# Seven products of quarter matrices in nine MLP rounds, and norms applied late at three junctions

## The reference

```
x = x + jnp.square(jax.nn.relu(rms_norm(x, norm_mlp) @ w_ff1)) @ w_ff2      # first block; then norm_final
...
for i in range(2):                                                          # second block
    h = rmsnorm(x, norm_mixer_pre[i])
    m = diff_attention(h, ...) if i == 0 else short_conv(h, ...)
    x = x + rmsnorm(m, norm_mixer_post[i])
    h = rmsnorm(x, norm_mlp_pre[i])
    x = x + rmsnorm(jnp.square(jax.nn.relu(h @ w_up[i])) @ w_down[i], norm_mlp_post[i])
```

## Time and profile before

| | |
|---|---|
| three runs | 2018.40, 2018.44, 2020.77 us; median 2018.44 |
| profiled execution | 2018.98 us, its span 2017.2 us |
| granted TensorE clock, mean | 0.998 |
| busy: TensorE, VectorE | 1991.0, 1051.5 us |
| DMA | 188.01 MB, mean 93 GB/s |

### The profile page before, as it was taken

The page is one execution under the profiler, slowest core; times in us unless marked ns, Lnnn a source line. Parts: engine busy times, 40 slices in busy tenths (PEclk is TensorE's granted clock), DMA queues, the critical chain, the costliest instruction groups (busy, mean ns, idle before and its releaser), DMA issues.

```text
span 2017.2 us, 23414 instructions
## 1 busy us (share of the span) xinstructions
PE 1991.0 (99%) x10007; PEld 1684.6 (84%) x10007; DVE 1051.5 (52%) x981; ACT 732.3 (36%) x786; POOL 153.7 (8%) x201
## 2 busy tenths in 40 slices
PE   9999999999999999999999999999999999999998
PEld 8788888888988888898888888888888888888886
DVE  7466586655533343477777634334464565333335
ACT  5464553352323232355555423132232333132222
POOL 0100150000100000030001200000020020000000
PEclk9999999999999999999999999999999999999999
DMA  5222122133332332332222333233223233223231
GB/s 192 90 78 69 63 65 82 63 105 114 105 105 86 102 104 84 105 102 69 74 63 84 107 103 104 84 104 100 88 84 105 84 104 115 94 95 104 86 102 63
DMA packets 98982, 188.01 MB, mean 93 GB/s; under 512 B 4350, under 2 KB 16784, under 8 KB 98896
## 3 DMA queue, kind: packets, MB, share of 16 engines
q1 hardware_dynamic: 94704, 176.17, 26.4%
q0 software_dynamic: 3904, 10.51, 1.8%
q10 hardware_dynamic: 288, 0.07, 0.0%
HBM read 183.59 MB, written 2.10 MB: 92 GB/s over the span
## 4 chain that ended last, share of the span: by engine, by line
PE 89%; DVE 5%; POOL 2%; ACT 2%; issue 1%; DMA 0%; DVEq 0%; POOLq 0%; ACTq 0%
PE ps L750 52%; PE ps L948 10%; PE ps L762 5%; PE ps L720 4%; PE ps L787 4%; PE ps L1199 2%; PE ps L1193 2%; PE ps L1146 1%; PE ps L821 1%; PE ps L1052 1%; PE ps L1218 1%; PE ps L1004 1%; PE ps L976 1%; PE ps L1342 1%; DVE w_lo L1900 1%
## 5 line engine op out<-in xcount | busy, mean ns | idle before, releaser
L1900 DVE TENSOR_TENSOR w_lo<-w_raw,w_hi 128x2048 fp32r<-128x2048 f32 x126 | 288.7, 2291 | 669.6 <-ACT w_hi L1400 669.6
L1400 ACT ACTIVATE w_hi<-w_raw 128x2048 fp32r<-128x2048 f32 x126 | 241.4, 1916 | 791.7 <-PE ps L750 662.1
L750 PE MATMUL ps<-a_hi,w_hi 128*128 128x512 f32 x880 | 342.4, 389 | 0.0
L750 PE MATMUL ps<-a_lo,w_hi 128*128 128x512 f32 x880 | 342.4, 389 | 0.0
L750 PE MATMUL ps<-a_hi,w_lo 128*128 128x512 f32 x880 | 342.3, 389 | 0.0
L750 PE MATMUL ps<-w_hi,h_hi 128*128 128x512 f32 x592 | 230.3, 389 | 0.0
L750 PE MATMUL ps<-w_lo,h_hi 128*128 128x512 f32 x592 | 230.3, 389 | 0.0
L750 PE MATMUL ps<-w_hi,h_lo 128*128 128x512 f32 x592 | 230.3, 389 | 0.0
L750 PEld LDWEIGHTS ps<-a_hi,w_hi 128*128 128x128 f32 x880 | 165.2, 188 | 34.3
L750 PEld LDWEIGHTS ps<-a_hi,w_lo 128*128 128x128 f32 x880 | 165.2, 188 | 34.2
L750 PEld LDWEIGHTS ps<-a_lo,w_hi 128*128 128x128 f32 x880 | 165.2, 188 | 34.1
(11 more groups left out here) (397 smaller groups left out, 3357.5 us busy)
## 6 DMA issues: line engine op xcount, KB each, us to landing
w_raw<-in_w_ff SPq DMA_DIRECT2D x32, 1024.0 KB, 5.2
w_raw<-in_mlp_w_up SPq DMA_DIRECT2D x32, 1024.0 KB, 5.4
w_raw<-in_mlp_w_down SPq DMA_DIRECT2D x32, 1024.0 KB, 5.1
w_raw<-in_w_in SPq DMA_DIRECT2D x24, 1024.0 KB, 5.1
w_raw<-in_attn_w_qkv SPq DMA_DIRECT2D x12, 1024.0 KB, 5.2
w_raw<-in_conv_w_in SPq DMA_DIRECT2D x12, 1024.0 KB, 5.1
w_raw<-in_w_proj_gla SPq DMA_DIRECT2D x4, 1024.0 KB, 5.1
w_raw<-in_w_out SPq DMA_DIRECT2D x4, 1024.0 KB, 5.1
```

Source lines behind the costliest of these rows:

```text
L750: last = mm(ps[:, bank0 + j], left, right, start=(k == 0 and x == 0), stop=(k == QUAD * quads - 1 and x == 2), skip_group_check=halves)
L1400: nc.scalar.activation(w_hi[:, s], w_raw[:, s], ACT.Copy).then_inc(hi_ready, 1)
L1900: tt(w_lo[:, s], w_raw[:, s], w_hi[:, s].bitcast(F32), ALU.subtract).then_inc(lo_ready, 1)
```

## The change

In the first three rounds of each MLP (`FAST`) the down product of 512x1024 by 1024x1024 is made of seven products of quarters (256 tokens x 512 features by 512x512) instead of eight, 24 matmuls each, in Winograd's form of Strassen's scheme. A round then has 11 quads: 4 of the up product and 7 for the products, of which four (numbers 5, 7, 8 and 9 of a round) are sums or differences of weight quarters. VectorE makes these sums in the raw slots (`weight_sums`); two more raw slots lie in `arena` (numbers 2 and 3 of `raw_at`), and SyncE loads a round's raw quads in the order 0, 1, 2, 3, 10, 4, 5, 6. It also makes four sums of hidden quarters and seven low parts, and adds the products into y with nine instructions of 128x1024. The square moves to ScalarE. Products 7, 9 and 10 accumulate onto an earlier product in PSUM and wait until VectorE has read it. The fourth round of each MLP stays as it was. The loops are unrolled.

At h_mlp1, h_conv and h_mlp2 the second scaling falls away: the residual times the gain goes into the next stage (`weighted`), and what depends on its scale is made good later. An MLP's output grows with the square of the factor and is normalized afterwards, so GpSimd only scales that norm's epsilon (`input_scale`). In conv_in two of the three projections are multiplied by the reciprocal of the variance, a row of 512 values that goes through DRAM to reach all partitions (`gate_c`). The order of the junction, of the last block and of the next first block changes with it (`begin_unscaled`). `clear_y` is gone: the first round writes y instead of adding. Some semaphores become the shared step counter.

The core of the diff (`loaded(n, s, last)` notes that quad n is loaded into slot s when the slot's earlier reader is through, and is read until quad `last` is split; `product` is 24 matmuls: two tiles of 128 tokens by four chunks by three parts):

```diff
+        raw_at = [w_raw[:, 0], w_raw[:, 1]] + [arena[:, 2048 * k:2048 * (k + 1)].rearrange("p (a n) -> p a n", a=QUAD) for k in range(2)]
+        h_raw = [qkf[:, 2048 * u:2048 * (u + 1)].rearrange("p (half a n) -> p half a n", half=2, a=4) for u in range(2)]
+        quarter = {"11": qkf[:, 0:1024], "21": qkf[:, 1024:2048], "12": qkf[:, 2048:3072], "22": qkf[:, 3072:4096],
+                   "s3": qkf[:, 4096:5120]}
...
+            n = 0
+            while n < n_quads:
+                mine = [name for name in MLPS if ph[name].q <= n < last_q(name)]
+                if not mine:
+                    loaded(n, n % 2, n)
+                    n += 1
+                    continue
+                for k in range(4):
+                    loaded(n + k, (n + k) % 2, n + k)
+                loaded(n + 10, 2, n + 10)
+                loaded(n + 4, n % 2, n + 9)
+                loaded(n + 5, (n + 1) % 2, n + 8)
+                loaded(n + 6, 3, n + 9)
+                for k, s_ in ((7, n % 2), (8, (n + 1) % 2), (9, n % 2)):
+                    slot[n + k] = s_
+                n += FAST_Q
...
+            def input_scale(name):
+                n = junctions[name][4]
+                pool.wait_ge(sumsq_ready, stat_count(name, n, TT - 1))
+                v = var[n % 2]
+                pstep(nc.gpsimd.tensor_scalar(v, sumsq[n % 2], EPS, None, ALU.add))
+                if name == "h_conv":
+                    pstep(nc.gpsimd.tensor_scalar(eps_in, v, EPS, None, ALU.mult))
+                else:
+                    pstep(nc.gpsimd.tensor_tensor(eps_in, v, v, ALU.mult))
+                    pstep(nc.gpsimd.tensor_scalar(eps_in, eps_in, EPS, None, ALU.mult))
...
+            input_scale("h_mlp1")
             refine_tiles("h_conv")
-            pool.wait_ge(chunk_lo, 4 + 2 * 16 + 8)
+            input_scale("h_conv")
+            nc.gpsimd.memset(small[:, 243:244], 0.0).then_inc(var_made, 1)
+            pool.wait_ge(inv_made, 1)
+            dma(scale_dram.rearrange("i p -> p i"), inv_var, allow_slow_non_contiguous=True).then_inc(scale_out, 16)
+            pool.wait_ge(scale_out, 16)
...
+                    turn_tile(name, 0)
+                    tile(2, 1).then_inc(tile_done, 1)
+                    turn_tile(name, 1)
+                    tile(3, 1).then_inc(quad_done, 1)
+                    return
...
+            def begin_unscaled(name, p, js, others):
+                bank0 = 4 * (p.b % 2)
+                s0, s1 = slot_of(p, 0, 0), slot_of(p, 0, 1)
+                pe.wait_ge(hi_ready, p.q + 1)
+                pe.wait_ge(turned_hi, turn_base[name] + 3)
+                half_pass(s0, 0, bank0, 0, 0, js)
+                pe.wait_ge(turned_lo, turn_base[name] + 4)
+                half_pass(s0, 0, bank0, 0, 0, others)
+                half_pass(s0, 0, bank0, 0, 1)
+                pe.wait_ge(lo_ready, p.q + 1)
+                half_pass(s0, 0, bank0, 0, 2)
+                pe.wait_ge(hi_ready, p.q + 2)
+                half_pass(s1, 1, bank0, 0, 0)
+                pe.wait_ge(banks_free, after_block[name])
+                turn_tile(name, 2)
+                half_pass(s1, 1, bank0, 0, 1)
+                pe.wait_ge(lo_ready, p.q + 2)
+                half_pass(s1, 1, bank0, 0, 2, (0, 1))
+                turn_tile(name, 3)
+                half_pass(s1, 1, bank0, 0, 2, (2, 3))
+                pe.wait_ge(turned_hi, turn_base[name] + 7)
+                half_pass(s0, 0, bank0, 1, 0)
+                pe.wait_ge(turned_lo, turn_base[name] + 8)
+                half_pass(s0, 0, bank0, 1, 1)
+                half_pass(s0, 0, bank0, 1, 2).then_inc(quad_done, 1)
+                for x in range(3):
+                    last = half_pass(s1, 1, bank0, 1, x)
+                last.then_inc(quad_done, 1)
...
+            def fast_round(name, r, chunks):
+                p, n = ph[name], fast_q(name, r)
+                b0, b1 = 4 * (p.b % 2), 4 * ((p.b + 1) % 2)
+                added = 9 * (FAST * MLPS.index(name) + r)
+                chunk, squares_ = chunks + PRODUCTS * r, exps_at(name, r)
+                for u in range(1 if r == 0 else 0, 2):
+                    if r:
+                        pe.wait_ge(y_added, added if u else added - 1)
+                    else:
+                        pe.wait_ge(banks_free, p.b)
+                    pe.wait_ge(lo_ready, n + 2 * u + 1)
+                    multiply(a_hi, a_lo, (n + 2 * u) % 2, 0, 4 * ((p.b + u) % 2), 2, False).then_inc(quad_done, 1)
+                    pe.wait_ge(lo_ready, n + 2 * u + 2)
+                    multiply_tiles((n + 2 * u + 1) % 2, 1, 4 * ((p.b + u) % 2)).then_inc(quad_done, 1)
+                for k, op, bank, start in ((4, 0, b0, True), (5, 1, b0 + 2, True), (6, 2, b1, True), (7, 3, b0, False),
+                                           (8, 0, b1 + 2, True), (9, 1, b0, False), (10, 2, b1 + 2, False)):
+                    if k == 4:
+                        pe.wait_ge(exp_ready, squares_ + 2)
+                    if k == 6:
+                        pe.wait_ge(exp_ready, squares_ + 4)
+                    if not start:
+                        pe.wait_ge(y_added, added + {7: 1, 9: 6, 10: 7}[k])
+                    pe.wait_ge(lo_ready, n + k + 1)
+                    pe.wait_ge(chunk_lo, chunk + k - 3)
+                    product(n + k, op, bank, start)
...
+            def relu(name, r, u, c):
+                bank = 4 * ((ph[name].b + u) % 2) + 2 * c
+                n = fast_q(name, r)
+                if c == 0 and (r or u):
+                    act.wait_ge(half_made, half_number(name, r, u))
+                else:
+                    act.wait_ge(quad_done, n + 2 * u + 2)
+                dst = h_raw[u][:, :, 2 * c:2 * c + 2]
+                src = ps[:, bank:bank + 2].rearrange("p a (half n) -> p half a n", half=2)
+                step(nc.scalar.activation(dst, src, ACT.Relu))
+                nc.scalar.activation(dst, dst, ACT.Square).then_inc(exp_ready, 1)
+            def operand(name, r, chunks, k, src, op, ready=None):
+                n = fast_q(name, r)
+                if ready is not None:
+                    act.wait_ge(chunk_f32, ready)
+                if k >= 8:
+                    act.wait_ge(quad_done, n + k - 3)
+                nc.scalar.activation(op_hi[op], quarter[src], ACT.Copy).then_inc(chunk_hi, 1)
+            def fast_round(name, r, chunks, f32):
+                n, sq, f = fast_q(name, r), exps_at(name, r), f32 + 3 * r
+                split_quad(n + 2)
+                relu(name, r, 0, 0)
+                relu(name, r, 0, 1)
+                act.wait_ge(exp_ready, sq + 2)
+                operand(name, r, chunks, 4, "11", 0)
+                split_quad(n + 3)
+                operand(name, r, chunks, 5, "s3", 1, f + 1)
+                split_quad(n + 4)
+                relu(name, r, 1, 0)
+                split_quad(n + 5)
+                relu(name, r, 1, 1)
+                act.wait_ge(exp_ready, sq + 4)
+                operand(name, r, chunks, 6, "12", 2)
+                operand(name, r, chunks, 7, "11", 3, f + 2)
+                split_quad(n + 6)
+                operand(name, r, chunks, 8, "21", 0)
+                split_quad(n + 7)
+                operand(name, r, chunks, 9, "22", 1)
+                split_quad(n + 8)
+                operand(name, r, chunks, 10, "12", 2, f + 3)
+                split_quad(n + 9)
+                split_quad(n + 10)
+                split_quad(n + 11)
+                split_quad(n + 12)
...
+            def weight_sums(name, r, ks):
+                n = fast_q(name, r)
+                a, b = n % 2, (n + 1) % 2
+                if 5 in ks:
+                    dve.wait_ge(raw_full[2], 16 * raw_fill[n + 10])
+                    dve.wait_ge(raw_full[b], 16 * raw_fill[n + 5])
+                    tt(raw_at[b], raw_at[2], raw_at[b], ALU.subtract).then_inc(w_summed, 1)
+                if 7 in ks:
+                    dve.wait_ge(lo_ready, n + 5)
+                    dve.wait_ge(w_summed, sum_number(name, r, 5))
+                    tt(raw_at[a], raw_at[a], raw_at[b], ALU.add).then_inc(w_summed, 1)
+                if 8 in ks:
+                    dve.wait_ge(lo_ready, n + 6)
+                    dve.wait_ge(w_summed, sum_number(name, r, 7))
+                    tt(raw_at[b], raw_at[2], raw_at[a], ALU.subtract).then_inc(w_summed, 1)
+                if 9 in ks:
+                    dve.wait_ge(raw_full[3], 16 * raw_fill[n + 6])
+                    dve.wait_ge(lo_ready, n + 8)
+                    dve.wait_ge(w_summed, sum_number(name, r, 8))
+                    tt(raw_at[a], raw_at[3], raw_at[a], ALU.subtract).then_inc(w_summed, 1)
+            def fast_round(name, r, chunks, f32, acc):
+                p, n = ph[name], fast_q(name, r)
+                b0, b1 = 4 * (p.b % 2), 4 * ((p.b + 1) % 2)
+                sq, f, chunk = exps_at(name, r), f32 + 3 * r, chunks + PRODUCTS * r
+                added = 9 * (FAST * MLPS.index(name) + r)
+                count = [added]
```

(143 more changed lines are left out.)

464 lines of the change are left out of this document (234 added, 230 removed).

## The result

The changed kernel takes 2027.43 us (median of 7 runs, 2023.99 to 2029.02) against 2018.64 us for the kernel before (7 runs, 2017.89 to 2020.77). The ratio is 1.0042, 95% interval 1.0031 to 1.0052: slower by 0.4%, twice what a measurement of this kernel can tell. The forecast was 2023.2 us, slower, with a range of 2013 to 2034. The profiled execution took 2026.71 us with a span of 2024.9, so 7.7 us more span than before.

What follows compares the result with a forecast made beforehand. TensorE, busy 99% of the span, was taken as the bound. Span 2017.2 - 49.0 + 59.1 + 2.7 - 8.0 = 2022.0 us; 1.8 more for the profiled execution, 0.5 less for the median: 2023.2 us, range 2013 to 2034.

Steps and rivals of the forecast that it cites:

- The products and the stalls: Nine fast MLP rounds: 49.0 us of matmuls saved, 59.1 of stalls and 2.7 of restarts added, +12.9 us.
- the walk: VectorE's fixed order timed through a fast round: TensorE waits 2.77, 2.38 and 1.42 us before products three, four and six.
- Pitches of 2.20 and 1.14: VectorE in fast rounds: one instruction of 128x2048 every 2.20 us, one of 128x1024 every 1.14 us.
- (a): Rival: VectorE's backlog in fast rounds is smaller than walked, 2014 us or less; chance 0.20, half only to no change.
- (b): Rival: VectorE's backlog in fast rounds is larger, 0.84 to 1.5 us more a round, 2031 to 2037 us; chance 0.12.
- The late norms: Junctions: h_conv -2.8 us, h_mlp2 -2.8 and h_mlp1 -2.4, together -8.0, with bounds of nothing and -13.3.
- Clearing y and the rest: Dropping two memsets beside an MLP's first block is worth nothing; unrolled loops and merged semaphores cost nothing a row shows.
- part 3: Small edits, among them conv_in's scales read back through DRAM, expected hidden: cost 0, upper end 2 us.
- Rival (d): The read-back of the scales is late and stalls conv_in, 2025 to 2029 us; chance 0.04.
- rival (c): TensorE's clock falls after stalls; one product a round at 1.2 GHz costs 49 us more, 2072 us; chance 0.02.

Runs made afterwards that it cites:

- e2: The changed kernel with the four weight sums replaced by one-column memsets, so its output is wrong: 2000.64 us.
- e7: The kernel of e1 with one move, VectorE's split of quad n+6 put ahead of the first product's addition into y: 2045.51 us.
- e3: The changed kernel with VectorE's and ScalarE's instructions in a fast round reordered, no work left out, and the early reciprocal: 1980.82 us.
- e5: The kernel of e1 with the four weight sums made on GpSimd, same order and waits: 2054.47 us.
- e6: The kernel of e3 with the four weight sums made on GpSimd: 2029.74 us.
- e4: The kernel before with the late norms alone, including the scaling in conv_in with its late reciprocal, MLP rounds and clearing of y untouched: 2012.01 us.
- e1: The changed kernel with VectorE's reciprocal of the variance moved ahead of conv_in's first two splits: 2021.46 us.

## Why the prediction was right, and where it wasn't

- **The products and the stalls** (-49.0, +59.1, +2.7): +12.9 forecast, +12.2 measured; a round of 88.5, measured 88.3 to 88.6. The waits end with VectorE's splits and lie where the walk put them, but for the sixth product's, which three rounds don't have. Their lengths are others than in the walk (2.70, 0.5 and 1.1 us, or 2.70 and 2.08, for 2.77, 2.38 and 1.42), because slow matmuls and the restarts fill the rest. The round comes out all the same: in six rounds VectorE's splits still set when the fourth and the sixth product start, and in three TensorE's slow stretch reaches past the time of the sixth one's split, by a few tenths. That the slow stretches fit in so was not foreseen, and in so far is luck. e2 and e7 change VectorE's queue alone, e3 that of ScalarE too, and the walk gives each one's sign and most of its size. It had the sign of e5 and e6 wrong: it let GpSimd and VectorE run side by side.
- **Pitches of 2.20 and 1.14**: held at a VectorE share far above before's. Rivals (a) and (b), which hung on them, are out. (By the parts given, the chance of slower adds up to 0.60 and of faster to 0.10, for 0.59 and 0.11.)
- **The late norms** (-8.0): h_conv -2.8 and h_mlp2 -2.85 as worked out, h_mlp1 -3.4 for -2.4, where I had counted four small waits; 0.3 of it lies in the attention before the junction. Two of the four roots in h_conv took 1.54 us, as the long one did before, and the junction wasn't the worse for it.
- **Clearing y and the rest, "worth nothing"**: the stretch to mlp0 is 1.1 us shorter, 0.5 in e4. Which edit gives it wasn't tried.
- **The failed step is part 3, the read-back of the scales**, "at the 3 to 4 us that I expect it is hidden. Cost 0, with 2 us as the upper end". The DMAs took 10.9 and 7.2 us (9.1 to 10.5 and 5.3 to 7.7 in the other runs), and the stretch lost 5.65 us in the profiled execution, 6.0 in the medians. I had bounded both by a row of a contiguous broadcast of 512 KB, 6.3 us. The write is of another kind, 512 pieces of four bytes. The same 2 KB as four rows of 512 bytes, though from DRAM to SBUF, took 1.9 us on the same queue:

```profile
arena<-in_b_gate_up POOLq DMA_DIRECT2D x1, 2.0 KB, 1.9
```

That the pieces make the write long is inferred; no run changed them alone. It isn't VectorE's work beside it: VectorE stood idle for the first 8 us of the 10.9. The read-back, of the row's kind and half its size, was above the row too, and why it varies stays open. Rival (d) named the mechanism at 2025 to 2029 and had 0.04. Without this step the sum would have been right within 1.7 us: e1 measured 2021.46.
- **The clock, rival (c)**: it said that a product a round at 1.2 GHz would cost 49 us. The granted clock did fall (0.98 over the round, where I expected 1.00 and had named anything lower as a sign of being wrong), as the Trainium skill's page "TensorE: Matmul & The Clock Gate", section "A second HAM failure mode: psum-queue depth-cycling", had warned. It fell for 2 to 5 us at a time (seven matmuls of 0.63 us above, eleven in a round of e7), worth 1.1 us (e2) to some 2.6 us (e7), and in the changed kernel's rounds the next wait swallowed that, or it took the place of the sixth product's wait. In conv_in, e2 and e7 nothing did.

## What to carry to other kernels

Fewer matmuls are worth what the engine that feeds them can follow: on average VectorE had room (56 us of 82), and its fixed order (with ScalarE's beside it, which e3 mends too) turned a saving of 49 us into a loss of 12 in the nine rounds. Walk the queue from the rows before moving work onto it, put what no one waits for behind what someone does, and price the order as a whole, since moving up a single split made it worse; with the order mended and the reciprocal early the same change gives 1.9%. And one row bounds a DMA poorly: the write was unlike the row of 6.3 us in direction and pieces and took 10.9, and the read-back, which was of its kind and half its size, still took 7.2.

## What the runs showed of the hardware

- A DMA on GpSimd's queue that writes 512 pieces of 4 bytes to DRAM took 9.1 to 10.9 us in eight kernels, and the 256 KB broadcast of them back 5.3 to 7.7 us.
- An addition or subtraction on GpSimd with both operands in SBUF (4.6 us for 128x2048) and a two-input instruction of VectorE in SBUF shut each other out for their full length (6.49 for 2.28 us, 5.50 for 1.22); one with an operand in PSUM isn't held (1.22).
- After waits of TensorE of 2.1 to 5.5 us the granted clock may fall to 1.2 GHz for 2 to 5 us. In e2 it fell after seven waits of 2.70 us and not after two of the same length and surroundings; in three rounds of the changed kernel it stayed through the wait of 2.70 us and fell after the one of 2.1 us that came 5.7 us later. In e3, whose longest wait in the rounds is 1.62 us, the granted clock over the span is 0.998, as before the change.
